# A two-block transformer kernel in float32: rope product merged, one product per latent head, the inverse's transpose rebuilt, query rows reversed and the bias lines written once

## The chip, the cores and the metric

The kernel runs on one core of one Trainium2 chip. The metric is the device time of one execution in microseconds, as the median of several runs; lower is better. Engines are named as in the profile: PE is TensorE, DVE is VectorE, ACT is ScalarE, POOL is GpSimd, SP is SyncE, which only issues DMAs here.

## The reference, cut to what matters

The first block normalises 272 rows (16 meta tokens, 256 tokens), projects them, and runs three kinds of attention side by side. The parts that the change touches:

```python
# latent attention (6 heads): a 64-wide part without and a 32-wide part with rotation
q_rot = rotate(q[..., MLA_NOPE:], cos, sin)
k_rot = rotate(k_rope, cos, sin)                 # one rotated key part for all heads
def rotate(x, cos, sin):
    x1, x2 = jnp.split(x, 2, axis=-1)
    return jnp.concatenate([x1 * cos - x2 * sin, x2 * cos + x1 * sin], axis=-1)

# differential (4 heads) and banded (6 heads): a bias that depends on q_pos - k_pos alone
bias = bias_tab[t5_bucket(q_pos[:, None], pos[None, :])]
logits = q @ k.T * scale + bias                  # then mask, softmax, @ v

# second block, gated delta rule: a strictly lower 128 x 128 matrix a per head and tile
t_mat = a + eye
u = triangular_solve(t_mat, v * beta);  w = triangular_solve(t_mat, k * beta * exp(gc))
```

All inputs and the output are float32. Two gated feed-forward blocks and the output projections take most of the arithmetic; the change does not touch them.

## The kernel before

The whole program is one stretch of code for each engine; order on an engine is program order, and semaphores tie the engines together.

**Weights.** SP streams the weights in 253 pieces of mostly 128 x 1024 floats (512 KB) into a ring of RAW = 5 buffers (L1017). It may load piece i only when piece i-5 has been split. ACT copies each piece to a rounded float32r half (L1044), DVE subtracts to get the rest (L1469), and both go to a ring of SPLIT = 6 pairs. A product then is three float32r matmuls for each k (L472 to L474). ACT and DVE keep AHEAD = 4 pieces ahead: before either waits for PE's result of piece n, it splits all pieces up to n+4, in order. So a piece that has not landed holds up everything that stands behind it on ACT, the evictions of PSUM banks among it.

**Input stage of block one.** PE turns the normalised rows (L490, L493), makes two lines of bias values for 10 heads (L614), then runs 13 feature products of 24 matmuls each, in the order `cq0 cq1 ckv dq0 dq1 dk0 dk1 sq0 sq1 sq2 sk krA krB`; after `dq1` come the sums of squares of the latents (L621 to L624), which need ACT's squares of `ckv` (L1152). Then come four pieces of token products (18 matmuls of 384 columns each) and, with the pieces `mla.*` used unsplit, six latent heads (L649, L651, L654) and the latent values (L659). `krA` holds the 32 rotary key features four times, `krB` the same features with halves swapped four times; DVE takes one times cos, the other times sin (L1660, L1662). For each latent head PE makes a 96-wide product and, in two further products, the swapped 32 features (L651) in other columns of the bank.

**Bias lines.** A head's bias is a line of 399 values; row q of the map is the line shifted by q. ACT copies both lines of 10 heads to SBUF (L1139) and writes them to DRAM, 128 times over (L1144), on its own DMA queue; POOL waits for that (L1391) and issues five reads (L1391 to L1395) in which each partition reads its own copy, at its own offset. DVE waits for the five reads before attention.

**PSUM.** Jobs take the 8 banks in turn. `opened` waits on PE until the bank's last user has been released, `closed` signals the result.

**Inverse of block two.** For 4 groups of 4 heads the inverse is built in levels 1 to 6. It keeps Y and its transpose X. In each level PE makes M = LT X for the four groups (L919), ACT copies M (L1329), then PE makes for each group X M and M Y (L933), and DVE subtracts them from X and Y (L1953); the last level updates Y alone. POOL masks the matrix for the next level (L1430). Nothing else runs beside it.

```python
for what in (["dx", "dy"] if lv < LEVELS - 1 else ["dy"]):   # inside: for g in range(4)
    a, b = (Yi, M) if what == "dx" else (M, Yi)
    last = mm(ps[:, s], a[:, g, s], b[:, g, s], start=True, stop=True)   # L933, 4 per job
```

Of the kernel before, what the change touches and what calls it, by code (L numbers as in the profile page):

```python
# [25 lines left out]
P = 128  # L26
# [42 lines left out]
NCONST = _place(CONST, [("ident", P), ("upper", P), ("negdist", 2 * P),  # L69
# [23 lines left out]
FEATURES1 = ["cq0", "cq1", "ckv", "dq0", "dq1", "dk0", "dk1", "sq0", "sq1", "sq2", "sk", "krA", "krB"]  # L93
# [41 lines left out]
def build(nc, consts, params, weights, x, meta, out, line_dram):  # L135
    ctx = ExitStack()
    with ctx:
# [202 lines left out]

        def heads_v(g, h):
# [91 lines left out]
        def _(pe):  # L433
# [49 lines left out]
            def transposes_of(src, name_of, gain_tiles=KD, meta=None):  # L483

                for k in range(gain_tiles):
# [6 lines left out]
                    for t in range(TT):  # L492
                        last = nc.tensor.transpose(ps[:, at + P * t:at + P * t + P], src[:, t, P * k:P * k + P], ident)  # L493
# [178 lines left out]
            transposes_of(y, lambda k: f"yT1_{k}")  # L672
# [235 lines left out]
            for lv in range(1, LEVELS):  # L908
                for g in range(4):
                    name = f"m{lv}_{g}"  # L910
                    ps = opened(name)
                    if lv == 1:
                        freed(pe, f"x0_{g}")
                    else:
                        freed(pe, f"dx{lv - 1}_{g}")
# [5 lines left out]
                for g in range(4):  # L921
                    freed(pe, f"m{lv}_{g}")
                    for what in (["dx", "dy"] if lv < LEVELS - 1 else ["dy"]):
                        name = f"{what}{lv}_{g}"
                        ps = opened(name)
                        if what == "dy" and lv > 1:
                            freed(pe, f"dy{lv - 1}_{g}")
                        if what == "dx" and lv > 1:
                            freed(pe, f"dy{lv - 1}_{g}")
                        for n in range(GH):  # L930
                            s = slice(P * n, P * n + P)
                            a, b = (Yi, M) if what == "dx" else (M, Yi)
                            last = mm(ps[:, s], a[:, g, s], b[:, g, s], start=True, stop=True)  # L933
                        closed(last, name)
# [91 lines left out]
        def _(act):  # L1026
# [113 lines left out]
            for v in range(2):  # L1140
# [3 lines left out]
            act.dma_start(line_dram.rearrange("q h n -> h q n"),  # L1144
                          att1["PTm"][0:BH, 0:2 * LINE].unsqueeze(1).to_broadcast([BH, P, 2 * LINE])).then_inc(sem("lines_out"), 16)
# [23 lines left out]
            for c in range(3):  # L1169
                full(act, f"p1_sq{c}")  # L1170
                release(A(sQ[:, c, :], bank_of(f"p1_sq{c}")[:, 0:SEQ], ACT.Copy, scale=SD ** -0.5), f"p1_sq{c}")
# [151 lines left out]
            for lv in range(1, LEVELS):  # L1323
                for g in range(4):
# [4 lines left out]
                    release(A(M[:, g, :], bank_of(name), ACT.Copy), name)  # L1329
            VN = cv[:, 0].rearrange("p h n -> p (h n)").rearrange("p (w h n) -> p w h n", w=2, h=NH2)  # L1330
# [46 lines left out]
        def _(pool):  # L1377
# [66 lines left out]
        def _(dve):  # L1444
# [214 lines left out]
            full(dve, "p1_krA")  # L1659
# [537 lines left out]
```

## Time and profile before

| | |
|---|---|
| median of 3 runs | 1138.11 us (1134.98 to 1143.31) |
| the profiled execution, its own time | 1133.66 us |
| its span, first to last instruction | 1131.8 us |
| mean granted TensorE clock | 0.947 |
| busy: PE, DVE, ACT, POOL | 1029.0, 631.1, 497.0, 179.0 us |
| weights read on SP's queue | 134.69 MB |
| the bias lines' write on ACT's queue | 3990 KB |

The profile is of one execution. "Busy" of PE counts matmuls in the pipeline, so a busy PE is not one at its peak. A row of windows gives the start and end of a stretch, its length, each engine's busy time with its number of instructions, the granted clock, the mean share of the 16 DMA engines that were busy, and the rate. Square brackets in a timeline hold the idle time before the instruction and what ended it. A float32 matmul (not float32r) shows as two instructions; a transpose shows as one.

### The profile page before, as it was taken

The page shows a single profiled execution, that of the slowest core. Times are in us where ns is not written, and L with a number is a line of the kernel's source. Part 1 is how long each engine was busy: PE and PEld are TensorE (multiplying, and loading weights), DVE is VectorE, ACT ScalarE, POOL GpSimd, SP SyncE. Part 2 cuts the span into 40 slices and gives each one's busy share as a digit, 9 for nine tenths or more (in the row PEclk, how much of TensorE's full clock was granted, in tenths as well). Part 3 has the DMA queues.
Part 4 walks back from the last instruction along what each step waited for, and adds up shares of the span by engine and source line. Part 5 has one row for each costly group of instructions (what it writes and reads, how often), then busy time and mean ns, then how long its engine had stood idle before and what let it go on. Part 6 is the DMA issues. An engine that isn't in the chain of part 4 may idle for free. (4 is left out here: it accounts for less than half of the span.)

```text
span 1131.8 us, 16805 instructions
## 1 busy us (share of the span) xinstructions
PE 1029.0 (91%) x6524; PEld 916.0 (81%) x6524; DVE 631.1 (56%) x1293; ACT 497.0 (44%) x919; POOL 179.0 (16%) x129
## 2 busy tenths in 40 slices
PE   4779678899999979999899999899899998999998
PEld 2676467699999969879788888799888777988996
DVE  3244455655555567458756459635485665555443
ACT  4242444554444344453465653322244445444441
POOL 0001000000000004003644202154000001332231
PEclk9899788899999988989889898989999998999999
DMA  6766200545655543363522101200055443555641
GB/s 231 152 149 169 74 1 2 204 152 187 215 178 164 177 149 107 136 224 123 176 75 76 38 2 54 75 1 1 1 171 202 166 156 125 186 186 191 202 166 56
DMA packets 40089, 144.24 MB, mean 127 GB/s; under 512 B 4346, under 2 KB 4730, under 8 KB 40010
## 3 DMA queue, kind: packets, MB, share of 16 engines
q1 hardware_dynamic: 37328, 134.69, 35.6%
q10 hardware_dynamic: 2154, 6.64, 3.4%
q0 software_dynamic: 528, 1.84, 0.5%
q8 instruction: 52, 0.85, 0.3%
q14 instruction: 27, 0.22, 0.1%
HBM read 138.02 MB, written 5.13 MB: 126 GB/s over the span
## 5 line engine op out<-in xcount | busy, mean ns | idle before, releaser
L1469 DVE TENSOR_TENSOR parts<-raw,parts 128x1024 fp32r<-128x1024 f32 (+1 forms) x228 | 290.2, 1308 | 207.9 <-ACT parts L1044 206.6
L1044 ACT ACTIVATE parts<-raw 128x1024 fp32r<-128x1024 f32 (+1 forms) x228 | 231.0, 1050 | 161.3 <-PE psum L474 101.7
L472 PE MATMUL psum<-hT,parts 128*128 128x256 f32 (+1 forms) x936 | 270.1, 289 | 5.3 <-DVE parts L1469 5.3
L473 PE MATMUL psum<-hT,parts 128*128 128x256 f32 (+1 forms) x936 | 268.5, 287 | 0.0
L474 PE MATMUL psum<-hT,parts 128*128 128x256 f32 (+1 forms) x936 | 266.6, 285 | 0.0
L472 PEld LDWEIGHTS psum<-hT,parts 128*128 128x128 f32 x936 | 180.5, 193 | 8.9 <-issue 7.6
L474 PEld LDWEIGHTS psum<-hT,parts 128*128 128x128 f32 x936 | 181.3, 194 | 0.0
L473 PEld LDWEIGHTS psum<-hT,parts 128*128 128x128 f32 x936 | 180.7, 193 | 0.6
L472 PE MATMUL psum<-parts,arena_r 128*128 128x512 f32 x344 | 136.3, 396 | 0.6 <-DVE parts L1469 0.4
L474 PE MATMUL psum<-parts,arena_r 128*128 128x512 f32 x344 | 135.9, 395 | 0.0
L473 PE MATMUL psum<-parts,arena_r 128*128 128x512 f32 x344 | 135.9, 395 | 0.0
L1086 ACT ACTIVATE arena<-arena,npeaks 128x128 f32<-128x128 f32 (+4 forms) x136 | 55.9, 412 | 70.4 <-DVE npeaks L1566 52.8
L472 PE MATMUL psum<-parts,hT 128*128 128x512 f32 (+2 forms) x200 | 78.0, 390 | 6.5 <-DVE parts L1469 6.5
L472 PEld LDWEIGHTS psum<-parts,arena_r 128*128 128x128 f32 x344 | 64.5, 187 | 16.6 <-DVE parts L1469 0.8
L473 PE MATMUL psum<-parts,hT 128*128 128x512 f32 (+2 forms) x200 | 77.2, 386 | 0.0
L474 PEld LDWEIGHTS psum<-parts,arena_r 128*128 128x128 f32 x344 | 64.5, 187 | 15.7
L474 PE MATMUL psum<-parts,hT 128*128 128x512 f32 (+2 forms) x200 | 77.2, 386 | 0.0
L473 PEld LDWEIGHTS psum<-parts,arena_r 128*128 128x128 f32 x344 | 64.6, 188 | 15.0
L1401 POOL TENSOR_SCALAR arena<-cbuf 128x256 f32<-128x256 f32 x16 | 14.5, 910 | 324.6 <-DVE X L1737 323.5
L1437 POOL TENSOR_TENSOR arena<-arena 128x512 f32<-128x512 f32 x16 | 16.6, 1040 | 268.8 <-ACT arena_r L1372 268.8
L472 PEld LDWEIGHTS psum<-parts,hT 128*128 128x128 f32 x200 | 39.1, 195 | 14.5 <-issue 4.1
L1408 POOL CAST parts<-raw 128x1024 fp32r<-128x1024 f32 x20 | 22.0, 1098 | 181.5 <-PE psum L474 180.3
(281 smaller groups left out, 1424.5 us busy)
## 6 DMA issues: line engine op xcount, KB each, us to landing
raw<-weights SPq DMA_DIRECT2D x248, 512.0 KB, 4.2
lines<-arena ACTq DMA_DIRECT2D x1, 3990.0 KB
raw<-weights SPq DMA_DIRECT2D x4, 384.0 KB, 20.6
X<-x SPq DMA_DIRECT2D x2, 512.0 KB, 5.9
out<-X SPq DMA_DIRECT2D x2, 512.0 KB, 2.6
arena<-lines POOLq DMA_DIRECT2D x1, 768.0 KB, 8.2
arena<-consts ACTq DMA_DIRECT2D x1, 671.0 KB, 8.2
arena<-lines POOLq DMA_DIRECT2D x1, 544.0 KB, 5.8
```

The lines of the kernel that those rows point to most:

```text
L472: mm(ps, a, c, start=start, stop=False)
L473: mm(ps, a, d, start=False, stop=False)
L474: return mm(ps, b, c, start=False, stop=stop)
L1044: signal(A(split_slot(name)[0], whole_piece, ACT.Copy), "first_parts")
L1086: signal(A(map_slot(g, E, n), map_slot(g, S, n), ACT.Exp, bias=npeaks[:, col:col + 1], accum_out=sums[:, col:col + 1]), tag)
L1401: nc.gpsimd.tensor_scalar(al[:, h, :], cst("negdist"), slope, None, ALU.mult).then_inc(sem("alibi"), 1)
L1408: nc.gpsimd.tensor_copy(first, whole_piece).then_inc(sem("pool_first"), 1)
L1437: nc.gpsimd.tensor_tensor(v, v, v, ALU.mult).then_inc(sem("squares2"), 1)
L1469: signal(V_.tensor_tensor(second, whole_piece, first.bitcast(F32), ALU.subtract), "split_vector")
```

## The change

- **Rope merge.** `krA` and `krB` become one piece `kr`: three times the 32 features, then once the swapped ones. DVE takes partitions 64 to 95 times cos and 96 to 127 times sin, both from one bank. The weight stream has one piece less (252), PE one feature product less.
- **One product per latent head.** The stationary operand is 128 wide, and the swapped features land in partitions 96 to 127; L651 and its two products are gone.
- **Transposed inverse.** X M is no longer made. After all four M Y of a level, PE transposes each updated Y (four transposes a group), and ACT copies it to X. DVE updates Y alone. The next level's M waits for that copy.
- **Reversed rows.** ACT evicts the differential and banded queries with the 128 rows of a tile in reverse order (a negative step when it reads PSUM). Row q then needs the line at offset +q instead of 127 - q. When y is transposed for the output projection, a matrix `flip` in place of the identity puts the rows of those heads back. `flip` adds 128 columns (64 KB) to the first constant load.
- **One copy of the lines.** ACT writes 10 x 798 floats (32 KB) once, and POOL's five reads take for partition p the shared line from offset p on; their sizes are as before.

```diff
-FEATURES1 = [... "sk", "krA", "krB"]
+FEATURES1 = [... "sk", "kr"]
...
+        def backwards(ps):
+            src = ps[:, 0:SEQ]
+            return bass.AP(tensor=src.tensor, offset=src.offset + P - 1, ap=[src.ap[0], [P, TT], [-1, P]])
...
                 for k in range(2):
-                    mm(ps[0:96, 0:SEQ], wq[h // 4][:, h % 4, k, 0:96], cn[:, k, real], start=(k == 0), stop=(k == 1))
-                for k in range(2):
-                    last = mm(ps[64:96, SEQ:2 * SEQ], wq[h // 4][:, h % 4, k, 96:128], cn[:, k, real], start=(k == 0), stop=(k == 1))
+                    last = mm(ps[:, 0:SEQ], wq[h // 4][:, h % 4, k, :], cn[:, k, real], start=(k == 0), stop=(k == 1))
...
-            transposes_of(y, lambda k: f"yT1_{k}")
+            flip = cst("flip")
+            transposes_of(y, lambda k: f"yT1_{k}", turn_of=lambda k: flip if k >= MH * MV // P else ident)
...
-                    if lv == 1:
-                        freed(pe, f"x0_{g}")
-                    else:
-                        freed(pe, f"dx{lv - 1}_{g}")
+                    freed(pe, f"x{lv - 1}_{g}")
...
                 for g in range(4):
                     freed(pe, f"m{lv}_{g}")
-                    for what in (["dx", "dy"] if lv < LEVELS - 1 else ["dy"]):
...
+                    name = f"dy{lv}_{g}"
+                    ps = opened(name)
+                    for n in range(GH):
+                        s = slice(P * n, P * n + P)
+                        last = mm(ps[:, s], M[:, g, s], Yi[:, g, s], start=True, stop=True)
+                    closed(last, name)
+                for g in range(4 if lv < LEVELS - 1 else 0):
+                    name = f"x{lv}_{g}"
+                    ps = opened(name)
+                    freed(pe, f"dy{lv}_{g}")
+                    for n in range(GH):
+                        s = slice(P * n, P * n + P)
+                        last = nc.tensor.transpose(ps[:, s], Yi[:, g, s], ident)
+                    closed(last, name)
...
-            act.dma_start(line_dram.rearrange("q h n -> h q n"),
-                          att1["PTm"][0:BH, 0:2 * LINE].unsqueeze(1).to_broadcast([BH, P, 2 * LINE])).then_inc(sem("lines_out"), 16)
+            act.dma_start(line_dram, att1["PTm"][0:BH, 0:2 * LINE]).then_inc(sem("lines_out"), 16)
...
-                release(A(dq[:, c, :], bank_of(f"p1_dq{c}")[:, 0:SEQ], ACT.Copy, scale=DQK ** -0.5), f"p1_dq{c}")
+                release(A(dq[:, c, :].rearrange("p (t n) -> p t n", t=TT), backwards(bank_of(f"p1_dq{c}")), ACT.Copy, scale=DQK ** -0.5), f"p1_dq{c}")
...
+                for g in range(4 if lv < LEVELS - 1 else 0):
+                    full(act, f"x{lv}_{g}")
+                    release(A(Xi[:, g, :], bank_of(f"x{lv}_{g}"), ACT.Copy), f"x{lv}_{g}")
...
             def shifted(head0, heads, v, m0, n):
-                return bass.AP(tensor=line_dram.tensor, offset=head0 * 2 * LINE + v * LINE + m0 + P - 1,
-                               ap=[[BH * 2 * LINE - 1, P], [2 * LINE, heads], [1, n]])
+                return bass.AP(tensor=line_dram.tensor, offset=head0 * 2 * LINE + v * LINE + m0,
+                               ap=[[1, P], [2 * LINE, heads], [1, n]])
...
-                    for what in (["dx", "dy"] if lv < LEVELS - 1 else ["dy"]):
-                        name = f"{what}{lv}_{g}"
-                        full(dve, name)
-                        tgt = (Xi if what == "dx" else Yi)[:, g, :]
-                        release(V_.tensor_tensor(tgt, tgt, bank_of(name), ALU.subtract), name)
+                    name = f"dy{lv}_{g}"
+                    full(dve, name)
+                    release(V_.tensor_tensor(Yi[:, g, :], Yi[:, g, :], bank_of(name), ALU.subtract), name)
```

## Rows read from the trace of the kernel before

**Rows 1.** Page, part 1: busy time, share of the span and instructions.

```profile
PE 1029.0 (91%) x6524; PEld 916.0 (81%) x6524; DVE 631.1 (56%) x1293; ACT 497.0 (44%) x919; POOL 179.0 (16%) x129
```

**Rows 2.** Windows over the input stage and the latent heads.

```profile
29.20:41.60 12.40, 12.40 (x102) 12.32 (x101) 3.71 (x4) 2.99 (x6) 0.00 (x0) 1.00 0.76 133
41.60:50.10 8.50, 0.13 (x2) 0.00 (x0) 0.30 (x1) 1.39 (x3) 0.00 (x0) 0.78 0.80 177
50.10:52.60 2.50, 2.41 (x6) 1.85 (x7) 0.92 (x1) 0.23 (x1) 0.00 (x0) 0.50 0.75 163
85.00:101.00 16.00, 13.29 (x73) 12.65 (x74) 5.70 (x8) 4.08 (x6) 4.68 (x5) 1.00 0.75 199
101.00:118.90 17.90, 17.90 (x67) 7.39 (x65) 8.11 (x19) 6.48 (x17) 0.00 (x0) 1.00 0.29 89
```

**Rows 3.** Timeline of ACT: the lines' write, and pieces that ACT waited for.

```profile
25.37 0.55 ACTq L1144 DMA_DIRECT2D lines<-arena  x1
48.71 1.06 ACT L1044 ACTIVATE parts<-raw 128x1024 fp32r<-128x1024 f32 x1 [14.97 <-DMA raw<-weights]
73.24 1.06 ACT L1044 ACTIVATE parts<-raw 128x1024 fp32r<-128x1024 f32 x1 [3.70 <-DMA raw<-weights]
78.19 1.06 ACT L1044 ACTIVATE parts<-raw 128x1024 fp32r<-128x1024 f32 x1 [3.62 <-DMA raw<-weights]
```

**Rows 4.** Timeline of POOL: the first read of the lines.

```profile
95.53 0.97 POOL L1391 DMA_DIRECT2D arena<-lines  x1 [92.79 <-DMA lines<-arena]
```

**Rows 5.** DMA queues, 20 to 130 us: packets, MB, share of 16 engines.

```profile
q10 hardware_dynamic: 1290, 4.09, 27.9%
q0 software_dynamic: 528, 1.84, 5.5%
```

**Rows 6.** Windows without the lines' write: what the DMA engines reach.

```profile
0.00:20.00 20.00, 4.71 (x18) 2.79 (x18) 7.43 (x29) 9.22 (x15) 2.21 (x8) 1.00 0.86 314
203.00:209.00 6.00, 6.00 (x28) 4.81 (x27) 3.28 (x5) 3.39 (x7) 0.00 (x0) 1.00 1.01 386
```

**Rows 7.** Timeline of DVE: start and end of its latent chain.

```profile
60.64 0.78 DVE L1647 TENSOR_SCALAR arena<-psum 128x272 f32<-128x272 f32 x2
68.94 2.35 DVE L1469 TENSOR_TENSOR parts<-raw,parts 128x1024 fp32r<-128x1024 f32 x2
```

**Rows 8.** Timeline of PE: one of the six latent heads.

```profile
103.51 1.10 PE L649 MATMUL psum<-arena,raw 128*96 128x256 f32 x4
104.54 1.05 PE L651 MATMUL psum<-arena,raw 128*32 128x256 f32 x4
105.52 0.67 PE L654 MATMUL psum<-arena,raw 128*64 128x272 f32 x2
```

**Rows 9.** Chain that ended last: start, us, what (one level; 16 transposes elsewhere).

```profile
743.80 7.15 PE psum L933 x64
750.94 3.57 PE psum L919 x32
875.90 1.75 PE psum L493 x16
```

**Rows 10.** Lines by form, 736 to 803 us: DVE, POOL, ACT beside the inverse.

```profile
L1953 DVE TENSOR_TENSOR arena<-arena,psum 128x512 f32<-128x512 f32 x44 | 30.3, 688 | 35.4 <-PE psum L933 35.4
L1430 POOL TENSOR_TENSOR arena<-arena 128x512 f32<-128x512 f32 x24 | 29.7, 1272 | 46.7 <-DVE arena L1946 23.5 <-PE psum L919 23.2
L1329 ACT ACTIVATE arena<-psum 128x512 f32<-128x512 f32 x24 | 14.3, 597 | 45.9 <-PE psum L919 45.9
```

**Rows 11.** Windows: clock in and behind 32 transposes, and later at half.

```profile
679.50:683.00 3.50, 3.50 (x35) 3.50 (x34) 3.01 (x6) 2.87 (x5) 0.00 (x0) 1.00 0.46 131
683.00:686.00 3.00, 3.00 (x16) 2.43 (x15) 2.80 (x4) 0.48 (x1) 0.00 (x0) 1.00 0.00 0
696.00:698.00 2.00, 1.01 (x8) 0.83 (x8) 2.00 (x4) 0.32 (x1) 0.00 (x0) 1.00 0.01 4
700.00:703.00 3.00, 3.00 (x16) 3.00 (x15) 2.72 (x10) 0.00 (x0) 0.00 (x0) 0.50 0.00 0
```

More of the change, by code:

```diff
@@ L66, in _place @@
     return at
-NCONST = _place(CONST, [("ident", P), ("upper", P), ("negdist", 2 * P),
+NCONST = _place(CONST, [("ident", P), ("flip", P), ("upper", P), ("negdist", 2 * P),
                         ("cmpbias", TT * NSH * NC), ("valid", TT), ("causal", ALL),
@@ L90, in _pieces @@
         WIDTHS[f"{name}.{n}"] = width
-FEATURES1 = ["cq0", "cq1", "ckv", "dq0", "dq1", "dk0", "dk1", "sq0", "sq1", "sq2", "sk", "krA", "krB"]
+FEATURES1 = ["cq0", "cq1", "ckv", "dq0", "dq1", "dk0", "dk1", "sq0", "sq1", "sq2", "sk", "kr"]
 for _n in FEATURES1:
@@ L481, in need, with transposes_of @@
                     freed(pe, arrivals.pop(k))
-            def transposes_of(src, name_of, gain_tiles=KD, meta=None):
+            def transposes_of(src, name_of, gain_tiles=KD, meta=None, turn_of=lambda k: ident):
                 for k in range(gain_tiles):
@@ L492, in transposes_of @@
                     for t in range(TT):
-                        last = nc.tensor.transpose(ps[:, at + P * t:at + P * t + P], src[:, t, P * k:P * k + P], ident)
+                        last = nc.tensor.transpose(ps[:, at + P * t:at + P * t + P], src[:, t, P * k:P * k + P], turn_of(k))
                     closed(last, name)
@@ L922, in _ @@
                     freed(pe, f"m{lv}_{g}")
-                    for what in (["dx", "dy"] if lv < LEVELS - 1 else ["dy"]):
-                        name = f"{what}{lv}_{g}"
[L925 to L934, printed above, removed]
+                    name = f"dy{lv}_{g}"
[12 more added lines that the diff above has]
+                    closed(last, name)
             Y4 = dn["Yi"].rearrange("p (t h n) -> p t h n", t=TT, h=NH2)
@@ L1170, in _ @@
                 full(act, f"p1_sq{c}")
-                release(A(sQ[:, c, :], bank_of(f"p1_sq{c}")[:, 0:SEQ], ACT.Copy, scale=SD ** -0.5), f"p1_sq{c}")
+                release(A(sQ[:, c, :].rearrange("p (t n) -> p t n", t=TT), backwards(bank_of(f"p1_sq{c}")), ACT.Copy, scale=SD ** -0.5), f"p1_sq{c}")
             full(act, "p1_sk")
@@ L1658, in _ @@
                                                op0=ALU.mult, op1=ALU.mult), "lat_norm")
-            full(dve, "p1_krA")
-            release(V_.tensor_tensor(rot[64:96, 0, :], bank_of("p1_krA")[64:96, 0:ALL], cos, ALU.mult), "p1_krA")
-            full(dve, "p1_krB")
-            release(V_.tensor_tensor(rot[64:96, 1, :], bank_of("p1_krB")[64:96, 0:ALL], sin, ALU.mult), "p1_krB")
-            freed(dve, "p1_krA")
-            freed(dve, "p1_krB")
+            full(dve, "p1_kr")
+            step(V_.tensor_tensor(rot[64:96, 0, :], bank_of("p1_kr")[64:96, 0:ALL], cos, ALU.mult))
+            release(V_.tensor_tensor(rot[64:96, 1, :], bank_of("p1_kr")[96:128, 0:ALL], sin, ALU.mult), "p1_kr")
+            settle()
+            freed(dve, "p1_kr")
             link(V_.tensor_tensor(rot[64:96, 0, :], rot[64:96, 0, :], rot[64:96, 1, :], ALU.add))
@@ L1670, in _ @@
                 step(V_.tensor_tensor(rot[64:96, 2, 0:SEQ], b_[64:96, 0:SEQ], cos[:, META:ALL], ALU.mult))
-                link(V_.tensor_tensor(rot[64:96, 3, 0:SEQ], b_[64:96, SEQ:2 * SEQ], sin[:, META:ALL], ALU.mult))
+                link(V_.tensor_tensor(rot[64:96, 3, 0:SEQ], b_[96:128, 0:SEQ], sin[:, META:ALL], ALU.mult))
                 dve.wait_ge(sem("q_nope"), h + 1)
@@ L2043, in shape_constants @@
     put("ident", j == i)
+    put("flip", j + i == P - 1)
     put("upper", j <= i)
@@ L2137, in laid_weights @@
     swapped = np.concatenate([kr[:, 16:], kr[:, :16]], 1)
-    feat = features(np.concatenate([cq, ckv, dq, dk, sq, sk] + [kr] * 4 + [swapped] * 4, 1))
+    feat = features(np.concatenate([cq, ckv, dq, dk, sq, sk] + [kr] * 3 + [swapped], 1))
     for n, what in enumerate(FEATURES1):
@@ L2192 @@
     out = nc.dram_tensor("out", (SEQ, D), F32, kind="ExternalOutput").ap()
-    lines = nc.dram_tensor("lines", (P, BH, 2 * LINE), F32, kind="Internal").ap()
+    lines = nc.dram_tensor("lines", (BH, 2 * LINE), F32, kind="Internal").ap()
     build(nc, ins["consts"], ins["params"], ins["weights"], ins["x"], ins["meta"], out, lines)
```

1 line of the change is left out of this document (removed).

## The prediction

> **What bounds the kernel now.** I read the page first: PE is busy for 1029.0 of 1131.8 us, DVE for 631.1, ACT for 497.0 [rows 1]. So a change pays where it takes work off PE while PE is the one waited for, or where PE stands idle. The chain of waits and windows over each stage that the diff touches then say which of these holds there. Three stages matter.
>
> *Input stage, 25 to 101 us.* In 29.2 to 41.6 PE is busy throughout: 102 matmuls in 12.40 us, 0.122 us each. Then it does nothing for 8.5 us, and the sums of squares behind that gap run at a granted clock of 0.50 [rows 2]. The gap ends when ACT evicts `ckv`, and ACT stood behind a weight piece: 14.97 us of wait. Later pieces come one per 4.95 us (78.19 less 73.24), with 3.6 us of waiting for DMA at each [rows 3], while PE needs 24 x 0.122 = 2.92 us for one. So weights bound this stage. What keeps them is the write of the bias lines: issued at 25.37 [rows 3], it releases POOL at 95.53 [rows 4], so it lasts 70 us, just the stage's length; it moves 4.09 MB and takes 27.9% of the 16 engines' time from 20 to 130 us [rows 5]. That is 58 GB/s, and 0.52 MB in 4.95 us is 106 GB/s for the weights beside it. Without it the engines moved 314 and 386 GB/s [rows 6], at which a piece takes 1.4 to 1.7 us.
>
> *Latent heads, 101 to 119 us.* PE is busy for all of 17.90 us, DVE for 8.11, ACT for 6.48, at full clock [rows 2]. PE bounds.
>
> *Inverse, 736 to 801 us.* The chain stays on PE: 7.15 us for the 32 products of X M and M Y, 3.57 for the 16 of M [rows 9]. DVE's 44 subtractions take 30.3 us in all, ACT's 24 copies 14.3, POOL's masks 29.7 [rows 10]. PE bounds here too.
>
> **Part by part.** *One copy of the lines, and the merged rope piece.* These two are costed together, as PE's time from 41.6 us to the end of the token pieces at 101.0. Up to 41.6 nothing changes: no product up to `dq1` waited for a piece. The write shrinks to 32 KB, so the piece that ACT waited 14.97 us for lands before ACT asks, and ACT has `ckv` squared before PE is through with `dq1`. What PE then has to do: the sums of squares, 2.5 us at half clock, 1.3 at full, which it keeps as there is no gap; seven feature pieces instead of eight, 7 x 2.92 = 20.4; four token pieces, which fill the last window before 101 (13.29 us busy with 73 matmuls, four pieces are 72) [rows 2], so 13.1. Sum 34.8, end at 76.4 instead of 101.0: 24.6 us less. Of this one feature product is 2.9 of PE work, the rest idle time and half clock given back. The upper end is some 1 us more (token pieces without the waits in that window).
>
> Who could be late instead of the DMA? ACT and DVE alternate through the latent chain, with pieces queued behind it on both. DVE began it at 60.64 and took up the next piece at 68.94: 8.3 us, table loads of ACT included [rows 7]. In the new order it starts when the sums end, at 42.9, so `sq2`, the first piece not split ahead of it (four ahead of `dq1` are), is ready at 42.9 + 8.3 + 1.2 = 52.4. PE wants it four pieces after 42.9, at 54.6. Margin 2.2 us, so I take nothing, and up to 5 us for the range.
>
> POOL's five reads move with the write: they were issued from 95.53 on and now follow it, at about 28 us. They are still 1.84 MB [rows 5], at 314 GB/s 5.9 us of the engines' time, now beside the pieces that PE needs at 43 to 55 us. By then five pieces (2.6 MB, 8.3 us) and the reads (5.9) are due, 14.2 us of transfer from 28 on, done near 42. Nothing by this sum, but the trace has no read in which all partitions take the same few KB, so the other end is the pace of the removed write (first rival). DVE needs them at the start of attention, some 45 us later.
>
> *One product per head.* L651 starts at 104.54 and the next work at 105.52: 0.98 us, gone six times, 5.9 us [rows 8]. What is left, 12.0 us of PE, stays above DVE's 8.11, whose instructions remain. The stationary operand grows from 96 to 128 columns; the trace shows no such product here, and I bound it between 0 and the 0.25 us of one of L649's instructions per head, 1.5 us, and take 0, since four instructions of L649 and four of L651 (a quarter as wide) cost nearly the same.
>
> *Transposed inverse.* In levels 1 to 5 the pair costs 7.15 us; M Y alone is one block of 3.57, and 16 transposes back to back took 1.75 elsewhere [rows 9]. Saved: 7.15 - 3.57 - 1.75 = 1.83, times five 9.1 us. New waits: x of group g waits for DVE's subtraction; that takes 0.69 us [rows 10], and group 3's transposes start 3 x 0.44 = 1.3 us after its product ends, so it is in time with some 0.4 us over. M of the next level waits for ACT's copy, 0.60 us each [rows 10]: copy 0 starts 0.44 us after the products and a semaphore's delay, done at about 1.3, PE asks at 1.75; copy 3 is done at about 3.1 and asked for at 4.4. ACT now has eight copies a level, 4.8 of 8.9 us, DVE four subtractions, POOL four masks, 5.1 us. All fit, POOL's included. Without that cover each tenth of a us late costs 0.5 in five levels.
>
> Does the clock hold? 32 transposes from 679.5 ran at a granted clock of 1.00, and the products behind them too [rows 11]; here only 16 stand between float32 products. It later fell to 0.50, behind a stretch in which PE was idle for half the time [rows 11], which the new inverse has not. The Trainium skill says otherwise: "TensorE: Matmul & The Clock Gate", Part 4 (PE-mode transpose), has it that transposes do not count as busy for the clock and do not bring full speed. By that rule the inverse may turn cold, which is the last rival; by the row it does not, and the sum goes by the row.
>
> *Reversed rows.* Five evictions by ACT read PSUM backwards. Between the trace's forward price and twice that (0.4 us more each) they hide: ACT is busy for 4.08 of 16 us at the end of the stage [rows 2]. `flip` replaces `ident` in as many transposes. Nothing in attention changes in number or size. The constant load grows by 64 KB ahead of the first transposes, at 314 GB/s 0.2 us, on the path: minus 0.2.
>
> **The sum.** 24.6 + 5.9 + 9.1 - 0.2 = 39.4 us. The profiled execution took 1133.7, 1.9 beside its span, so it would take 1094.3. It is 4.4 below the median of the runs, which I keep as offset: 1138.1 - 39.4 = 1098.7 us.
>
> **Rivals.**
> - *The reads take the write's place.* For: all partitions now read the same few KB, and the removed transfer shows how one slow transfer starves the weights. Against: they moved through at high rates before, with rows of the same length. At 58 GB/s 1.84 MB last 31 us, in which 6.3 pieces come at 4.95 instead of 2.92 us: 12.7 us back, 1111; with the 8.5 us gap too, 1120.
> - *The latent chain on ACT and DVE is late* by up to 5 us, or x and M stall in the inverse by a few tenths per level: 1099 to 1105. For: margins of 2.2 and 0.4 us. Against: the durations above are of whole chains, gaps included.
> - *The weights have their own pace*, whatever the write does. Then the stage gives only one piece, 4.95 us, and the total is 1138.1 - 4.95 - 5.9 - 9.1 + 0.2 = 1118. Against: 314 and 386 GB/s [rows 6].
> - *The clock falls in the inverse*, which ends on the other side. PE's work there would be 5 x (3.57 + 3.57 + 1.75) + 7.15 = 51.6 us at full clock, and at half clock twice that: 1098.7 + 51.6 = 1150. It cancels the whole gain once PE is cold for 39.4 / 51.6 = 76% of the stage. Against: rows 11, in which 32 transposes kept the clock [rows 11]. That page's rule speaks for it.
>
> **How the numbers follow.** Forecast (all three gains come, 1090 to 1103 with the 8 us spread of the runs shown): 0.72. Reads contend: 0.12. Late chain: 0.09. Weights' own pace: 0.04. Cold inverse: 0.03. The range 1090 to 1112 takes in the forecast, the late chain and the nearer half of the contending reads; left out are 0.06 + 0.04 + 0.03 and the tails of the spread. One per cent, about what a measurement of this kernel can tell from no change, is 11.4 us: only the cold inverse is slower by more, and little of the cases near 1120 reaches 1126.7. Faster 0.94, same 0.04, slower 0.02.
>
> **What the profile would show.** Input: the lines' write done in a few us and POOL's reads issued near 28 us; no gap of PE near 42; no piece waited for by ACT for over 2 us; the last token product near 76 instead of 101. Heads: six starts of L649's successor 1.6 us apart instead of 2.6. Inverse: levels of 8.9 us instead of 10.7 at granted clock 1.00, 16 transposes in 1.75 us, DVE with 24 subtractions. Attention and all between 205 and 736 us should only be shifted, by some 30 us. The prediction is wrong if weights still come at 4 us and more, if ACT or DVE in place of DMA holds PE before 76 us, or if the clock in the inverse is below 1.

## The result, and the profile after

| | before | after |
|---|---|---|
| median, us | 1137.23 (1134.98 to 1143.31, 4 runs) | 1094.09 (1089.91 to 1097.89, 4 runs) |
| ratio, 95% interval | | 0.9614 (0.9582 to 0.9646) |
| span of the profiled execution, us | 1131.8 | 1090.5 |
| mean granted TensorE clock | 0.947 | 0.953 |

The forecast was 1098.7 us with a range of 1090 to 1112. Four milestones split the two spans: where the latent heads begin on PE, where attention begins (DVE's first step of it), where the inverse begins (POOL's first mask, at 736.13 and 704.38, 1.41 us before the first M on PE), and the end.

| stretch, us | before | after | difference | forecast |
|---|---|---|---|---|
| start to the first latent head | 100.96 | 75.77 | -25.2 | -24.6 + 0.2 |
| latent heads and values, to attention | 19.82 | 14.06 | -5.8 | -5.9 |
| attention to the inverse (not changed) | 615.35 | 614.55 | -0.8 | 0 |
| inverse and the rest | 395.67 | 386.12 | -9.55 | -9.1 |

The page of the changed kernel, part 1 (busy time, share, instructions). PE has lost 128 instructions and 25.4 us, ACT has gained 9.6 us, as the copies of X are now its own [rows 1]:

```profile
PE 1003.6 (92%) x6396; PEld 896.3 (82%) x6396; DVE 616.8 (57%) x1272; ACT 506.6 (46%) x938; POOL 178.6 (16%) x129
```

**Input stage.** Timeline of ACT: the lines' write, and the two longest waits for a piece.

```profile
25.49 0.55 ACTq L1147 DMA_DIRECT2D lines<-arena  x1
38.77 1.06 ACT L1047 ACTIVATE parts<-raw 128x1024 fp32r<-128x1024 f32 x1 [2.40 <-DMA raw<-weights]
64.03 1.06 ACT L1047 ACTIVATE parts<-raw 128x1024 fp32r<-128x1024 f32 x1 [2.58 <-DMA raw<-weights]
```

Timeline of POOL: the first read of the lines.

```profile
27.45 0.97 POOL L1396 DMA_DIRECT2D arena<-lines  x1 [24.71 <-DMA lines<-arena]
```

The write takes 2 us where it took 70 [rows 4], and the wait of 14.97 us [rows 3] is gone. Windows over the stage (start:end, length, busy time and instructions of PE, PEld, DVE, ACT, POOL, granted clock, DMA share, GB/s):

```profile
29.20:41.60 12.40, 12.40 (x102) 12.36 (x101) 6.19 (x6) 6.26 (x12) 2.50 (x4) 1.00 1.00 326
41.60:50.00 8.40, 8.40 (x66) 8.20 (x66) 4.21 (x7) 6.96 (x9) 0.00 (x0) 1.00 0.57 209
50.00:60.00 10.00, 10.00 (x86) 10.00 (x84) 8.07 (x11) 4.83 (x9) 0.00 (x0) 1.00 0.52 161
60.00:70.00 10.00, 10.00 (x67) 10.00 (x66) 4.50 (x6) 2.19 (x3) 0.00 (x0) 1.00 0.45 142
```

Where PE was busy for 0.13 of 8.5 us at a clock of 0.78 [rows 2], it is now busy throughout at 1.00. The column of the DMA shows that PE sets the pace from 41.6 on: the engines move 142 to 209 GB/s at a share of about one half, because nobody asks for more.

Timeline of DVE: the start of its latent chain, and the piece behind it.

```profile
43.64 0.78 DVE L1652 TENSOR_SCALAR arena<-psum 128x272 f32<-128x272 f32 x2
51.96 1.22 DVE L1474 TENSOR_TENSOR parts<-raw,parts 128x1024 fp32r<-128x1024 f32 x1
```

The chain takes 8.32 us again [rows 7]. It starts at 43.64, not at 42.9, because DVE first splits a piece (42.50 to 43.64) whose copy on ACT had waited 1.30 us for DMA. So `sq2` is ready at 53.2. PE asks four pieces after its sums of squares end at 42.35, which by their prices (two of 3.0, two of 2.9 us) is near 54.2.

DMA queues from 20 to 90 us (packets, MB, share of 16 engines) and the largest read (KB, us to landing):

```profile
q1 hardware_dynamic: 2275, 7.35, 30.9%
q0 software_dynamic: 528, 1.84, 9.3%
...
arena<-lines POOLq DMA_DIRECT2D x1, 768.0 KB, 12.2
```

POOL's reads from the one shared copy take 9.3% of 70 us, 6.5 us of the engines, against 5.5% of 110 = 6.05 with a copy for each partition [rows 5]. Reading the same few KB in all partitions costs little more here than reading a copy for each.

**Latent heads.** Timeline of PE: the sums of squares, and two heads.

```profile
41.18 0.62 PE L626 MATMUL psum<-arena,ones 128*128 128x272 f32 x2
...
75.77 1.02 PE L654 MATMUL psum<-arena,raw 128*128 128x256 f32 x4
76.72 0.67 PE L657 MATMUL psum<-arena,raw 128*64 128x272 f32 x2
77.33 1.13 PE L654 MATMUL psum<-arena,raw 128*128 128x256 f32 x4
78.39 0.67 PE L657 MATMUL psum<-arena,raw 128*64 128x272 f32 x2
```

From 76.72 to 78.39 are 1.67 us for a head. Before, a head took 2.6: the 0.98 us of L651 stood between the other two [rows 8].

**Inverse.** The chain that ended last (start, us, what): one level.

```profile
712.06 3.57 PE psum L928 x32
715.63 1.75 PE psum L936 x16
717.38 3.57 PE psum L920 x32
```

Windows over the five levels with the transposes, the same columns as above, and lines by form from 704 to 762 us:

```profile
712.10:756.50 44.40, 44.40 (x402) 44.40 (x401) 13.76 (x20) 22.26 (x40) 21.96 (x18) 1.00 0.00 1
```

```profile
L1955 DVE TENSOR_TENSOR arena<-arena,psum 128x512 f32<-128x512 f32 x24 | 16.5, 688 | 40.1 <-PE psum L928 40.1
L1334 ACT ACTIVATE arena<-psum 128x512 f32<-128x512 f32 x20 | 10.3, 603 | 17.1 <-PE psum L936 17.1
L936 PE MATMUL psum<-cbuf,arena 128*128 128x128 f32 x80 | 9.6, 273 | 0.0
L928 PE MATMUL psum<-arena 128*128 128x128 f32 x192 | 22.4, 275 | 0.0
```

A level takes 3.57 + 1.75 + 3.57 = 8.89 us instead of 10.72 [rows 9]. PE is busy for 44.40 of 44.40 us at a granted clock of 1.00, and neither L936 nor L928 waited for anybody.

### The profile page after: what moved, and what is told of

It is laid out like the page before. It is cut to its first block and busy times, and to the rows that moved or that the text cites. A ratio compares the mean times of both kernels' runs of the same rounds, so it can differ in the third digit from the quotient of the medians.

```text
span 1090.5 us, 16547 instructions
## 1 busy us (share of the span) xinstructions
PE 1003.6 (92%) x6396; PEld 896.3 (82%) x6396; DVE 616.8 (57%) x1272; ACT 506.6 (46%) x938; POOL 178.6 (16%) x129
## 5 line engine op out<-in xcount | busy, mean ns | idle before, releaser
L477 PE MATMUL psum<-hT,parts 128*128 128x256 f32 (+1 forms) x928 | 265.1, 286 | 0.0
L478 PE MATMUL psum<-hT,parts 128*128 128x256 f32 (+1 forms) x928 | 264.2, 285 | 0.0
L479 PE MATMUL psum<-hT,parts 128*128 128x256 f32 (+1 forms) x928 | 262.3, 283 | 0.0
L477 PEld LDWEIGHTS psum<-hT,parts 128*128 128x128 f32 x928 | 176.5, 190 | 3.3 <-issue 1.9
L479 PEld LDWEIGHTS psum<-hT,parts 128*128 128x128 f32 x928 | 177.8, 192 | 0.0
L478 PEld LDWEIGHTS psum<-hT,parts 128*128 128x128 f32 x928 | 176.8, 191 | 0.5
L1415 POOL TENSOR_TENSOR parts<-raw,parts 128x1024 fp32r<-128x1024 f32 x20 | 49.3, 2465 | 1.6
## 6 DMA issues: line engine op xcount, KB each, us to landing
arena<-lines POOLq DMA_DIRECT2D x1, 768.0 KB, 12.2
```

Of the source, the lines that this page charges most:

```text
L477: mm(ps, a, c, start=start, stop=False)
L478: mm(ps, a, d, start=False, stop=False)
L479: return mm(ps, b, c, start=False, stop=stop)
L1415: nc.gpsimd.tensor_tensor(second, whole_piece, first.bitcast(F32), ALU.subtract)\
```

## The experiments

My theory was the sum of the prediction: the 128-fold write starved the weights; the heads and the inverse each cost what their PE instructions cost. Rivals: a slow pace of the weights whatever the write does, contention from the reads, late ACT and DVE, a colder clock in the inverse.

### One part at a time: e1 to e4

Each applies one part of the change to the kernel before, all else as it was.

**e1: one copy of the lines and reversed rows** (`flip` included).

> The kernel before with the bias lines written once, the reversed differential and banded rows that this needs, and the flip matrix; the rope pieces krA and krB, two products per latent head and the old inverse stay. My theory: the write of 4.09 MB starves the weights; without it PE bounds the input stage. PE then needs 41.6 + 1.3 (sums of squares) + 8 x 2.92 (feature pieces) + 13.1 (token pieces) = 79.4 us instead of 101.0 for the last token product, so 21.6 us less, 0.2 back for the longer constant load: about 21.4 us below the kernel before, ratio 0.981; no gap of PE near 42 us. Rival, the weights have their own pace of 4.95 us a piece whatever the write does: no change within 1 us. Rival, the reads of one shared copy take the place of the write: 12.7 us or more of the gain is missing, and pieces still come over 4 us apart between 28 and 60 us.

**e2: the rope merge alone.**

```diff
-FEATURES1 = [... "sk", "krA", "krB"]
+FEATURES1 = [... "sk", "kr"]
```

> The kernel before with the rope merge alone: one weight piece and one feature product less, the 128 copies of the lines still written. If the weights bound the stage while the write lasts, the saving is one piece at its starved pace, 4.9 us, ratio 0.9957, with PE still idle near 42 us. If PE's work is what counts, it is 2.9 us, ratio 0.9974. If the stage ends only with the write itself at 95.5 us whatever PE has to do, it is under 2 us.

**e3: one product per latent head alone.**

> The kernel before with one 128-wide product per latent head and nothing else. PE bounds that stage: six heads start 1.63 us apart instead of 2.61, 5.9 us less, ratio 0.9948. If the wider stationary operand costs the upper bound, 4.4 us, ratio 0.9961. If DVE or ACT bounds the stage instead, heads start at least 1.9 us apart and less than 4.3 us is gained.

**e4: the transposed inverse alone.**

> The kernel before with the inverse's transpose rebuilt by PE transposes, nothing else. If PE stays the bound at a granted clock of 1.00, levels 1 to 5 take 8.9 us instead of 10.7: 9.1 us less, ratio 0.992. If the new waits (transpose behind DVE's subtraction, M behind ACT's copy) bite, PE shows idle time before the transposes or before M and the gain is below 7 us. If transposes let the clock fall, as a rule has it, the stage shows a clock below 1 and the kernel is up to 42 us slower than the kernel before.

| | median, us | ratio, 95% interval | trace: attention starts | inverse to end |
|---|---|---|---|---|
| before, 26 runs beside them | 1136.48 | | 120.78 | 395.67 |
| e1 | 1118.27 (1110.26 to 1119.8) | 0.9852 (0.9818 to 0.9886) | 99.18 (-21.6) | 395.64 |
| e2 | 1133.41 | 0.9964 (0.9942 to 0.9985) | 119.94 (-0.8) | |
| e3 | 1132.16 | 0.9959 (0.9940 to 0.9978) | 115.20 (-5.6) | |
| e4 | 1128.91 | 0.9929 (0.9900 to 0.9958) | | 386.01 (-9.66) |

Window over PE's old gap in e1:

```profile
41.60:50.00 8.40, 8.40 (x65) 8.17 (x65) 4.97 (x8) 6.85 (x10) 0.00 (x0) 1.00 0.53 211
```

The write alone closes the gap: 21.6 us, half of the whole gain. (The medians differ by only 18.2 us, and the ratio's interval, 13 to 21 us, just misses the 21.4 expected. Its repeats spread over 9.5 us, told of below, and the lowest, 1110.26, is the one with the trace. So the 21.6 rests on the stage in the trace, not on the times.) Heads (5.6 against 5.9) and inverse (9.66 against 9.1) give alone what they give together.

The rope merge alone gives little, since the write still holds the weights. Timeline of ACT in e2:

```profile
48.45 1.06 ACT L1044 ACTIVATE parts<-raw 128x1024 fp32r<-128x1024 f32 x1 [15.28 <-DMA raw<-weights]
...
53.44 1.06 ACT L1044 ACTIVATE parts<-raw 128x1024 fp32r<-128x1024 f32 x1 [3.36 <-DMA raw<-weights]
```

The same 15 us of waiting as before [rows 3]. Its trace shows 0.8 us at the start of attention, its times 4.1 us (1.7 to 6.6), one piece at the starved pace being 4.95; in e5 below, where a piece is missing beside the same write, the heads begin 3.5 us earlier than before. What the merge is worth under the old write stays open between these.

### The write back in, whole and in a quarter: e5, e6

The changed kernel, with 128 or 32 copies written; POOL still reads the first.

```diff
-            act.dma_start(line_dram, att1["PTm"][0:BH, 0:2 * LINE]).then_inc(sem("lines_out"), 16)
+            act.dma_start(line_dram[0:32].rearrange("q h n -> h q n"),
+                          att1["PTm"][0:BH, 0:2 * LINE].unsqueeze(1).to_broadcast([BH, 32, 2 * LINE])).then_inc(sem("lines_out"), 16)
```

> The changed kernel with its 128 copies of the lines written again (same source, same queue, same place); POOL's reads take the shared first copy as in the changed kernel. My theory: the starvation comes back whole. PE is idle again near 42 us, pieces come 4.9 us apart, and of the gain in the input stage only the one piece is left: some 19.6 us above the changed kernel, 1138 - 19.9 = about 1117 to 1118, ratio to the kernel before 0.983. If the reads' shared source or the reversed rows gave the gain and not the smaller write, it stays near the changed kernel, 1094 to 1098.

> The changed kernel with 32 copies written, 1.02 MB. At the pace seen before (58 GB/s) the write lasts 17.5 us, from 25.5 to 43. Starvation only in that time: the piece that the eviction of the latents waits for was 15 us late with 128 copies, when it landed at 48; it now lands between 40 and 44, so PE loses a few us near 42 and nothing later: 2 to 6 us above the changed kernel. If any write of this shape costs in proportion to its bytes, a quarter of 19.6, 4.9 us; if only the queueing up to the end of the first pieces counts, as much as 8 us.

e5: 1117.89 us, ratio 0.9835 (0.9798 to 0.9872), within what was expected. Timeline of its ACT, then of its POOL:

```profile
48.46 1.06 ACT L1047 ACTIVATE parts<-raw 128x1024 fp32r<-128x1024 f32 x1 [15.62 <-DMA raw<-weights]
53.45 1.06 ACT L1047 ACTIVATE parts<-raw 128x1024 fp32r<-128x1024 f32 x1 [3.36 <-DMA raw<-weights]
```

```profile
95.44 1.56 POOL L1397 DMA_DIRECT2D arena<-lines  x1 [92.70 <-DMA lines<-arena]
```

The write alone brings back the wait of 15 us, the pace of one piece per 4.9 to 5.0 us, and the POOL read at 95.44; attention starts at 111.52 instead of 89.83. With all other parts of the change in place this is 21.7 us, the same as e1 took away. So the write, and not the reads' layout or the number of pieces, is the cause. The reads here take the one shared copy and the kernel pays for the write all the same.

e6: 1105.60 us, ratio 0.9717 (0.9675 to 0.9759), 11.5 above the changed kernel, in the trace 7.65 at the start of attention. I had expected 2 to 6: a miss. Its POOL (read at 43.58) and ACT:

```profile
43.58 0.97 POOL L1397 DMA_DIRECT2D arena<-lines  x1 [40.83 <-DMA lines<-arena]
```

```profile
44.57 1.06 ACT L1047 ACTIVATE parts<-raw 128x1024 fp32r<-128x1024 f32 x1 [11.33 <-DMA raw<-weights]
```

Its PE, and a window behind the gap:

```profile
46.06 1.25 PE L626 MATMUL psum<-arena,ones 128*128 128x272 f32 x2 [4.85 <-ACT arena L1155]
```

```profile
46.00:52.00 6.00, 5.94 (x21) 5.27 (x22) 4.47 (x6) 4.58 (x7) 1.84 (x3) 0.52 0.96 319
```

The write ended after 18 us, a quarter of 70, as expected; the piece landed at 44.57 and PE stood for 4.85 us. What I left out is the clock: behind the gap it is 0.52, so the sums of squares take 2.47 us (to 48.53) instead of 1.17, and the next 13 products 3.30 us (48.53 to 51.83) instead of 1.83 (42.35 to 44.18 in the changed kernel). The sums start 4.88 us later than in the changed kernel; 4.88 + 1.30 + 1.47 = 7.65, as seen. Over a third of the price of this stall is the clock behind it. For the other 4 us of the measured 11.5 the input stage has no place; the stretch behind it, in which nothing differs, took 5.7 us more in this trace (below).

### What the write itself is limited by: e7, e9, e10

The changed kernel, with an additional write of 4.09 MB to a spare tensor at the start of attention, read from 10 partitions (as the removed one), from 128, or from 16. POOL waits for its end. Its data are constants that nobody uses. (The diff is of the first of the three, with P = 128.)

```diff
+            act.dma_start(spare.rearrange("q h n -> h q n"),
+                          cbuf[0:BH, 0:2 * LINE].unsqueeze(1).to_broadcast([BH, P, 2 * LINE])).then_inc(sem("spare_out"), 16)
             attention(G1, {})
```

> The changed kernel, and in addition a write of the same shape as the removed one (128 copies of 10 rows of 798 floats, to a spare tensor, result unused) issued by ACT just before attention, at about 88 us, where SP's queue moves next to nothing after some 8 us; POOL waits for it and then clears a small tile. If the write is slow by itself, whatever runs beside it, it again lasts 50 to 70 us, at 58 to 80 GB/s, and ends near 150. If it was the weights that slowed it, it is done in 13 to 20 us. Either way attention does not need it: the time stays within 2 us of the changed kernel, unless the first weights of the output projection, which load at about 88 to 95 us, are late by it.

> The changed kernel with the additional write at the start of attention, as in the run with the late write from 10 rows (it lasted 67 us there, 50 GB/s, with nothing else moving for most of it). The same 4.09 MB in the same 1280 runs of 3192 bytes, result unused, but read from all 128 partitions (10 runs each) instead of from 10 partitions (128 runs each). If reading from few partitions, or the few DMA engines that serve them, made it slow, it lasts 12 to 20 us, at 200 to 340 GB/s. If writes of 3192-byte runs to DRAM are slow as such, it again lasts over 50 us.

> As the run with 128 rows, with the same bytes and runs read from 16 partitions (80 runs each). If the pace goes by partition, the time falls by 10/16, from 67 to about 42 us. If it goes by how many of the 16 engines take part, and 16 rows bring in all of them, again 42 us (0.41 us a run and engine); if the low partitions share a path whatever their number, it stays near 67 us. A time near 13 us would say that only the uneven split over 10 rows was slow.

Timeline of POOL, first instruction behind the write (issued at 88.29, 88.32 and 88.42), and queues and issues from 88 to 155 us. With 10 partitions:

```profile
155.34 0.10 POOL L1406 MEMSET mark<- 128x8 f32 x1 [123.75 <-DMA spare<-cbuf]
```

```profile
q10 hardware_dynamic: 1290, 4.09, 48.5%
...
raw<-weights SPq DMA_DIRECT2D x4, 512.0 KB, 19.3
```

With 128 partitions:

```profile
108.07 0.10 POOL L1405 MEMSET mark<- 128x8 f32 x1 [76.58 <-DMA spare<-cbuf]
```

```profile
q10 hardware_dynamic: 1296, 4.09, 15.6%
...
raw<-weights SPq DMA_DIRECT2D x4, 512.0 KB, 8.6
```

With 16 partitions (the window is one in which no weights move):

```profile
131.34 0.10 POOL L1406 MEMSET mark<- 128x8 f32 x1 [99.48 <-DMA spare<-cbuf]
```

```profile
q10 hardware_dynamic: 1296, 4.09, 51.6%
...
raw<-weights SPq DMA_DIRECT2D x4, 512.0 KB, 15.4
```

```profile
110.00:130.00 20.00, 17.04 (x119) 14.47 (x122) 10.29 (x56) 9.12 (x33) 0.00 (x0) 0.89 0.96 103
```

The same bytes, in the same 3192-byte runs to the same tensor, take 67 us from 10 partitions, 42.9 from 16 (42 expected) and 19.7 from 128 (12 to 20 expected). From 10, 128 runs of each partition in 67 us are 0.523 us a run; from 16, 80 in 42.9 are 0.536: the same pace, 3192 bytes in 0.53 us, which is 6 GB/s if it is counted for each partition that is read. With 16 partitions the 16 DMA engines show as busy (0.96) while they move 103 GB/s; e9 reaches 358 GB/s from 90 to 107 with as many packets. So it is neither the number of packets, nor the DRAM side, nor the number of engines that take part (busy to 0.94 in e9, 0.96 in e10): it is reading much from few partitions. Two things stay open. A limit that neighbouring partitions share would give the same ratio of 10 to 16, as long as the fullest group is full in both, so the 6 GB/s need not belong to a single partition. And fewer partitions also meant that the same bytes were read over more often (128, 80 and 10 times); no run read different bytes from few partitions. The write is not only slow, it holds engines: from 10 partitions alone the 16 engines are busy to 0.49 while they move 54 GB/s (120 to 150 us), from 16 to 0.96 at 103 GB/s, and four weight pieces of 512 KB land in a median of 19.3 and 15.4 us beside it, and in 5.1 in the changed kernel. That is the starvation of the removed write, seen apart from the input stage.

e7 measured 1096.74 us, ratio 0.9644 (0.9615 to 0.9672), 2.7 us above the changed kernel and not told apart from it: the weights that it delays are not needed at the start of attention. e9 and e10 were run once each, 1090.1 and 1083.65 us. The slow transfer costs by where it stands: the same bytes from the same number of partitions cost 21.7 us in the input stage (e5).

### Does the clock fall with more transposes: e8

The changed kernel with each of the 16 transposes of a level done four times over.

```diff
                     for n in range(GH):
                         s = slice(P * n, P * n + P)
-                        last = nc.tensor.transpose(ps[:, s], Yi[:, g, s], ident)
+                        for _again in range(4):
+                            last = nc.tensor.transpose(ps[:, s], Yi[:, g, s], ident)
```

> The changed kernel with each transpose of levels 1 to 5 of the inverse made four times over into the same place, 64 in a row instead of 16 (same values). If the clock holds, each level takes 3.57 + 3.57 + 7.0 = 14.1 us instead of 8.9 at a granted clock of 1.00: 5 x 5.25 = 26.2 us above the changed kernel. If a run of transposes lets the clock fall, the row of windows over the runs of transposes or the products behind them shows 0.5, and the time is 35 to 60 us above it.

1121.09 us, ratio 0.9859 (0.9820 to 0.9898). From the inverse to the end it is 412.79 us, 26.7 more, with 26.2 expected at full clock. Its chain, and a window over the 64 transposes and one over the products behind them:

```profile
721.76 6.99 PE psum L937 x64
728.74 3.57 PE psum L920 x32
```

```profile
721.80:728.70 6.90, 6.90 (x66) 6.90 (x65) 0.68 (x1) 1.79 (x3) 0.00 (x0) 1.00 0.01 2
728.80:732.30 3.50, 3.50 (x34) 3.50 (x33) 0.00 (x0) 2.37 (x4) 2.58 (x3) 1.00 0.00 0
```

64 transposes at 0.109 us each, the price of the 16, and 3.57 us for the products behind, as without them. The clock stays at 1.00 in both. "TensorE: Matmul & The Clock Gate" of the Trainium skill, Part 4 (PE-mode transpose), has it that transposes do not count as busy for the clock. The measurement decides, and it says otherwise as far as keeping the clock goes, for float32 transposes in 7 us at a time between products; longer ones were not tried. Whether transposes bring the clock up is not shown: at its start the changed kernel does nothing but transposes on PE from 15.40 to 22.04, and its products of 272 columns still take 0.23 us each from 25.20 to 28.14, later 0.125.

### Two further steps: e11, e12

e11: ACT normalises the second tile before it splits the first weight piece, so that PE can begin earlier. e12: e11, and the eight pieces of `z0` and `z1` are split by ACT and DVE as the others are, not by POOL.

```diff
-            first_parts(1)
             second_tile("1", jn)
+            first_parts(1)
...
-BY_POOL = {n for n in PIECES if "." in n and n.split(".")[0] in ("dv1", "dq0", "dq1", "z0", "z1")}
+BY_POOL = {n for n in PIECES if "." in n and n.split(".")[0] in ("dv1", "dq0", "dq1")}
```

> The changed kernel with two steps of ACT exchanged at the start: it normalises the second tile of rows before it copies weight piece 0, for which it waited until 13.16 us while the norm's factor was there at 12.4. PE's first transpose should start near 14.0 instead of 15.4 us, limited by DVE's meta rows, and all behind it 1.2 to 1.4 us earlier, ratio to the changed kernel 0.9988. If piece 0 is then split too late for the first product, PE waits near 24 us and the gain is gone.

> The kernel with the exchanged steps, and in addition the eight weight pieces z0 and z1 split by ACT and DVE instead of POOL. Beside POOL's subtractions DVE's steps on 16 columns took up to 2.3 us instead of 0.17, in the chain behind which PE idles for 1.8 us at 663 to 665 and less elsewhere. If that idle time is worth it, 2 to 5 us less than the kernel with the exchanged steps. If the eight splits (8 x 1.2 us on DVE, in order, with DVE busy over 90% there) weigh more, it is slower by up to 8 us, and PE waits for DVE in 650 to 700 us.

e11: 1099.38 us, ratio 0.9661 (0.9634 to 0.9688). PE begins at 13.97 instead of 15.40, but attention starts only 0.66 us earlier (89.17), where 1.2 to 1.4 was expected: a miss. Products of 272 columns took 0.23 us each until 28.5 in e11 and until 28.1 without it, then 0.125: part of the earlier start is spent at the slow pace. There is no gain in the time; the median is 5.3 us above the changed kernel's, with a stretch in which nothing differs 7.7 us longer (below). The window of e11 over that pace, in whose 29 instructions are 22 such products, begun from 23.37 to 28.30:

```profile
20.00:28.50 8.50, 8.50 (x29) 5.79 (x29) 3.90 (x6) 5.70 (x8) 2.48 (x3) 1.00 0.11 24
```

e12: 1086.83 us (1086.33 to 1091.14), ratio 0.9585 (0.9564 to 0.9605), 7.3 us below the changed kernel; the intervals of the two ratios still overlap. It is the lowest median of those run more than once. Against e11 it is 12.6 us lower, where 2 to 5 was expected: a miss in the time. In the trace 4.0 us of it are found where they were looked for; 9.1 lie in the stretch from attention to L850 (556.53 against 565.60 us). Six of the eight pieces are split there, but the stretch took from 552.18 (e10) to 565.60 us (e11) in kernels that leave them to POOL, so the trace can't tell what they are worth in it. For the 4.0, timeline of DVE in the changed kernel, and of POOL beside it:

```profile
655.46 0.17 DVE L1505 TENSOR_TENSOR st<-st 128x16 f32<-128x16 f32 x1
655.67 2.27 DVE L1506 SCALAR_TENSOR_TENSOR st<-st 128x16 f32<-128x16 f32 x1
```

```profile
655.47 2.43 POOL L1415 TENSOR_TENSOR parts<-raw,parts 128x1024 fp32r<-128x1024 f32 x1
```

Timeline of DVE in e12:

```profile
653.25 0.18 DVE L1506 SCALAR_TENSOR_TENSOR st<-st 128x16 f32<-128x16 f32 x1
```

A step on 16 columns takes 0.18 us alone and ends at 657.94, with POOL's subtraction at 657.90, when that runs beside it. Steps of this kind form a chain (square root and norms of the query rows) that PE waits for; without POOL's pieces, the stretch from the 32 transposes of L850 to the inverse takes 52.64 us, with them 56.65 in the changed kernel and 56.64 in e11: 4.0 us. "SBUF — State Buffer" of the Trainium skill, section "Who interferes with whom", tells of a port that VectorE and GpSimd share; the trace agrees, with 2.27 against 0.18 us.

Not all of the 4.0 us is the wait itself. In the changed kernel PE stands idle for 1.81 us in this stretch (before 665.24), and from 667.7 to 674.5, with its 32 products, the granted clock is 0.58. e10 has POOL's pieces and the same 1.81 us of idle time, but there the clock stays at 1.00 (657.7 to 666). Timeline of PE in the changed kernel, then in e10:

```profile
667.76 6.51 PE L869 MATMUL psum<-cbuf,gl 128*128 128x128 f32 x32
```

```profile
661.92 3.82 PE L870 MATMUL psum<-cbuf,gl 128*128 128x128 f32 x32
```

In e10 the whole stretch takes 54.13 us. So about 1.5 us of the 4.0 are what POOL's pieces cost by themselves, and 2.5 the clock behind the wait, which fell in one kernel and not in the other.

### The spread of the repeats

From the start of attention to the inverse all kernels but e12 do the same work on the engines (e7, e9 and e10 have the additional write beside it). The traces have it in 615.35 (before), 614.55 (after), 613.58 (e1), 618.37 (e2), 619.95 (e3), 615.98 (e4), 619.30 (e5), 620.25 (e6), 621.14 (e8) and 622.24 us (e11), and with the additional write in 618.57 (e7), 612.22 (e9) and 606.31 us (e10). Over this stretch the granted clock is 0.94 in e10, 0.92 in the kernel before and 0.91 in e11. Two windows, each from 15 to 30 us behind the start of attention, of the changed kernel and of e11:

```profile
104.83:119.83 15.00, 10.39 (x62) 8.59 (x62) 9.96 (x53) 5.55 (x23) 0.00 (x0) 0.89 0.00 1
```

```profile
104.17:119.17 15.00, 11.94 (x52) 10.23 (x53) 6.64 (x36) 4.29 (x18) 0.00 (x0) 0.56 0.00 1
```

At a granted clock of 0.89 PE did more in less busy time than at 0.56. PE stands idle for a fifth to a third of these windows in short breaks, and the clock comes out differently from kernel to kernel; over the whole stretch the times differ by up to 8.7 us, and by 15.9 with e10. This explains why a gain read from one trace and the difference of two medians may be several us apart (e6: 7.65 and 11.5). What decides how the clock comes out was not tried.

## Why the prediction was right

The median came 4.6 us below the forecast, 43.1 under its before against 39.4 foreseen (interval of the ratio: 40 to 48); span against span the gain is 41.3. By its steps:

- **What bounds the input stage.** Right: e1 and e5 remove and bring back 21.6 and 21.7 us by the write alone. I had put one piece in the sum for the merge (2.9 of 24.6); e1, with the piece kept, leaves 3.6 for it (25.2 - 21.6). The tie of a late piece to PE's gap was read rightly too: in e5 the wait of 15.62 us for DMA is back before it.
- **PE's time from 41.6 to the heads.** Forecast end 76.4, seen 75.77. `dq1` ended at 41.18, not 41.6; the sums of squares took 1.2 us at full clock (1.3 foreseen), the rest 33.4 (33.5).
- **Late chain.** Did not come: chain of 8.3 us as taken, a start 0.7 us later than I had it (behind a piece that was waited for), the margin thus nearer 1 than 2 us.
- **Reads contend.** They cost PE nothing: 6.5 us of the engines against 6.05. Beside them all engines were busy (1.00 from 29.2 to 41.6) and the largest read landed in 12.2 us instead of 8.2; ACT waited for a piece by 2.40 and, when the reads were long done, by 2.58 us, where I had said none over 2; PE did not notice either time. That mark was set too tight.
- **Weights' own pace.** Refuted by e1, where the heads begin 21.6 us earlier with all 253 pieces; in the changed kernel weights and reads together come at 326 GB/s from 29.2 on.
- **Heads.** 0.95 us gone per head, 5.8 us in all with 5.9 foreseen. The wider stationary operand cost next to nothing: 1.66 us between heads, 1.63 by the sum, so 0.2 us in six heads.
- **Inverse.** First M to last M Y took 54.3 us instead of 63.4: 9.1, as forecast to the tenth. A further 0.4 us of the stretch lies behind it; I did not trace it.
- **Clock in the inverse.** It held at 1.00, and e8 shows that four times as many transposes do not change that.
- **Constant load.** Foreseen 0.2 us; PE's first instruction came at 15.40 instead of 15.29, 0.1 us.
- **Size of the median's gain.** Of the 3.7 us by which it exceeds the sum, 1.9 are in the span (0.8 in the input stage, 0.8 in the unchanged stretch, 0.4 in the inverse, less 0.1 in the heads), the rest lies within the repeats' spread. That the total fits this well is in part luck: the prediction had nothing for the unchanged stretch, which came out 0.8 us shorter here and 7.7 us longer in e11. What the runs support is the gain by stage.

What the prediction had in no number is the share of the clock in the gap: it took half clock for the sums of squares alone [rows 2]. Here this cost nothing, since all of the gap went and PE's work was rightly priced at full clock; for e6, where part of it stayed, the same omission made me miss.

## What to carry to other kernels

When a prefetch ring runs dry, look for another transfer under way at that time and work out its rate: a broadcast from few partitions can keep the DMA engines busy at a fraction of their rate (from 16 partitions 103 GB/s, from 128 it was 358), and making its data small or its moment harmless frees the stage. A price in PE time is safe where the window shows PE busy throughout on both sides of the edit and each consumer has its margin counted; where part of a stall stays, add the clock behind it. Differences of a few us in a kernel with a stretch of idle and busy PE need many repeats or a comparison of traces by stage.

## What was not expected of the hardware

- A DMA that reads the same rows over and over from 10 or 16 partitions went at about 6 GB/s per partition (0.53 us for a run of 3192 bytes; whether the limit is that of a partition or of a group is open), and weight pieces beside it land in 15.4 to 19.3 us instead of 5.1. The removed write was slow for reading so much from so few partitions, not for its 4 MB: from 128 partitions as many bytes took 19.7 us.
- 64 float32 transposes in a row, 6.99 us, between products, left the granted clock at 1.00.
- A 16-column step of DVE took up to 2.3 us instead of 0.18 beside a two-input operation of POOL, and ended with it.
- The same idle time of 1.81 us was followed by a granted clock of 0.58 in the changed kernel and of 1.00 in e10.
- Up to 28.5 us the trace of e11 shows a granted clock of 1.00 (its window above) while products of 272 columns took 0.23 us, twice their later price of 0.125. The granted clock alone does not tell the pace there.
